# Attention with two queues of block moves: from four and twelve per head to eight and eight

## The reference

```python
def attend_blocks(q, k_all, v_all):              # 16 heads of 128, 4 key heads, 256 queries, 512 keys
    def one(qblk):
        s = jnp.einsum('bqkgd,btkd->bkgqt', qblk, k_all).astype(jnp.float32) * scale
        p = jax.nn.softmax(s, axis=-1).astype(v_all.dtype)
        return jnp.einsum('bkgqt,btkd->bqkgd', p, v_all)
    ...
    y_a = (jax.nn.sigmoid(o_a) * h * jax.nn.silu(z_a)) @ w_ba
    y_b = (o_attn * jax.nn.silu(z_b)) @ w_bb
    return (jax.nn.sigmoid(g_a) * y_a + jax.nn.sigmoid(g_b) * y_b) @ w_out
```

## Time and profile before

| | |
|---|---|
| median of 3 runs | 3128.25 us (3126.66 to 3133.57) |
| the profiled execution's own time | 3128.57 us |
| its span (first to last instruction) | 3126.6 us |
| busy: PE, DVE, ACT, POOL | 3104.6, 2145.0, 1464.9, 722.5 us |
| the attention's steps on PE | 2510 to 2673 us of the span |

### The profile page before, as it was taken

The page is one execution under the profiler, slowest core; times in us unless marked ns, Lnnn a source line. Parts: engine busy times, 40 slices in busy tenths (PEclk is TensorE's granted clock), DMA queues, the critical chain, the costliest instruction groups (busy, mean ns, idle before and its releaser), DMA issues.

```text
span 3126.6 us, 41616 instructions
## 1 busy us (share of the span) xinstructions
PE 3104.6 (99%) x14804; PEld 2561.7 (82%) x14804; DVE 2145.0 (69%) x2591; ACT 1464.9 (47%) x1805; POOL 722.5 (23%) x1127
## 2 busy tenths in 40 slices
PE   9999999999999999999999999999999999999998
PEld 8888888888777888888988888888888877888887
DVE  6888875556887678887786764655666866555556
ACT  5444444444337444444443545545455554445443
POOL 1111107947660301111012000000000577110000
PEclk9999999999999999999999999999999999999999
DMA  8999986556443789999888667546876777777754
GB/s 257 293 314 303 295 275 216 195 191 198 147 140 110 230 244 297 298 297 312 260 293 263 198 186 211 175 143 171 173 153 188 207 189 174 210 206 212 228 183 155
DMA packets 441565, 687.10 MB, mean 220 GB/s; under 512 B 138120, under 2 KB 146576, under 8 KB 440768
## 3 DMA queue, kind: packets, MB, share of 16 engines
q1 hardware_dynamic: 384176, 567.21, 57.8%
q0 software_dynamic: 39824, 115.72, 14.8%
q10 hardware_dynamic: 17408, 2.10, 0.5%
HBM read 647.93 MB, written 2.10 MB: 208 GB/s over the span
## 4 chain that ended last, share of the span: by engine, by line
PE 97%; DVE 1%; ACT 1%; POOL 0%; DMA 0%; issue 0%; SPq 0%; DVEq 0%; POOLq 0%; ACTq 0%
PE acc L301 25%; PE acc L303 25%; PE acc L302 25%; PE acc L1052 3%; PE pst L1052 3%; PE acc L1053 2%; PE pst L1054 2%; PE pst L1053 2%; PE acc L1054 2%; PE pst L2866 1%; PE pst L2545 1%; PE pst L2855 1%; PE pst L1682 0%; PE pst L2378 0%; PE pst L2547 0%; PE acc L324 0%
## 5 line engine op out<-in xcount | busy, mean ns | idle before, releaser
L249 DVE TENSOR_TENSOR w_lo<-w_raw,w_hi 128x1024 fp32r<-128x1024 f32 x1059 | 1312.1, 1246 | 807.8 <-ACT w_hi L242 800.5
L242 ACT ACTIVATE w_hi<-w_raw 128x1024 fp32r<-128x1024 f32 x1059 | 1120.3, 1060 | 1449.3 <-PE acc L303 1080.8
L301 PE MATMUL acc<-w_hi,act_hi 128*128 128x512 f32 (+1 forms) x3360 | 1319.0, 393 | 0.5 <-DVE act_lo L401 0.3
L303 PE MATMUL acc<-w_hi,act_lo 128*128 128x512 f32 (+1 forms) x3360 | 1302.9, 388 | 0.0
L302 PE MATMUL acc<-w_lo,act_hi 128*128 128x512 f32 (+1 forms) x3360 | 1302.6, 388 | 0.0
L301 PEld LDWEIGHTS acc<-w_hi,act_hi 128*128 128x128 f32 x3360 | 631.7, 188 | 131.1 <-issue 5.3
L303 PEld LDWEIGHTS acc<-w_hi,act_lo 128*128 128x128 f32 x3360 | 631.6, 188 | 127.7
L302 PEld LDWEIGHTS acc<-w_lo,act_hi 128*128 128x128 f32 x3360 | 631.9, 188 | 125.0 <-issue 1.4
L729 POOL DMA_DIRECT2D mod_ring<-in_w_mod x160 | 113.8, 711 | 831.1 <-DVE pst L749 765.8
L749 DVE SCALAR_TENSOR_TENSOR pst<-mod_ring,c_act,pst 128x512 f32<-128x512 f32 x285 | 214.6, 753 | 6.1 <-DMA mod_ring<-in_w_mod 0.7
L1052 PE MATMUL pst<-w_hi,g_hi 128*128 128x512 f32 x344 | 134.4, 391 | 0.0
(11 more groups left out here) (477 smaller groups left out, 2539.1 us busy)
## 6 DMA issues: line engine op xcount, KB each, us to landing
w_raw<-in_w_in SPq DMA_DIRECT2D x400, 512.0 KB, 4.0
w_raw<-in_ffn_w_down SPq DMA_DIRECT2D x168, 512.0 KB, 4.4
w_raw<-in_ffn_w_gate SPq DMA_DIRECT2D x160, 512.0 KB, 5.1
w_raw<-in_ffn_w_up SPq DMA_DIRECT2D x160, 512.0 KB, 6.7
mod_ring<-in_w_mod POOLq DMA_DIRECT2D x160, 512.0 KB, 6.1
w_raw<-in_w_out SPq DMA_DIRECT2D x64, 512.0 KB, 4.1
w_raw<-in_w_branch_a SPq DMA_DIRECT2D x32, 512.0 KB, 3.8
w_raw<-in_w_branch_b SPq DMA_DIRECT2D x32, 512.0 KB, 4.5
```

The costliest lines, as they stand in the source:

```text
L242: act.activation(weight_tiles(s)[0], w_raw[:, s % SLOTS, :], ACT.Copy).then_inc(w_hi_done, 1)
L249: dve.tensor_tensor(lo, w_raw[:, s % SLOTS, :], hi.bitcast(F32), ALU.subtract).then_inc(w_lo_done, 1)
L301: pe.matmul(o, xh, wh, start=k == 0, stop=False)
L303: mm = pe.matmul(o, xl, wh, start=False, stop=k == 2 * nch - 1)
```

## The change

The table of groups per queue changes. Queue 0 is ACT's, queue 1 is POOL's; each group stands for four DMAs of a head. The semaphore targets in `A2_MOVED` follow from the table.

```diff
-        A2_GROUPS = ((3,), (0, 1, 2))
+        A2_GROUPS = ((2, 3), (0, 1))
         A2_MOVED = [16 * 4 * len(groups) for groups in A2_GROUPS]
```

## The result

| | before | after |
|---|---|---|
| median, chip of the first comparison | 3128.20 us (3126.66 to 3133.57, 4 runs) | 3151.56 us (3147.54 to 3153.15, 4 runs) |
| ratio, 95% interval | | 1.0076 (1.0064 to 1.0088) |
| a second comparison, another chip | 3126.70 us (19 runs) | 3151.45 us (4 runs), 1.0081 (1.0064 to 1.0097) |
| profiled execution: time, span | 3128.57, 3126.6 us | 3147.54, 3145.7 us |

A forecast was written before the change was run, and what follows sets the result against it. PE was taken to bound the kernel, busy 3104.6 of 3126.6 us. Opening 1.83, even part 6.56, evictions 1.84 and end 2.25 sum to 12.48 us: 3140.7 against 3128.25, range 3133.5 to 3148.5.

The forecast's parts named there:

- 0.36 + 10 x 0.62: Even part, heads 3 to 13: PE stalls 0.36 us once, then 0.62 for each head, 6.56 us in all.
- the end's 0.77: End of the stage: PE's output behind head 15's eight issues and eviction comes a further 0.77 us late.
- 5.33 from exp to rounding: ACT with eight issues: the next rounding starts 5.33 us behind exp, in place of 2.70 with four.
- the hole in the opening: PE's idle 3.14 us ahead of the second output, with a slow clock behind; forecast to change owner and grow by 1.83.
- the threshold of 2.18 us: Even part: a rounding on ACT may be 2.18 us late before PE waits.
- 1.48 behind head 14: End of the stage: PE's output behind head 14's late rounding comes 1.48 us late.
- The rule of the Trainium skill that gave a rival: Rival: POOL was the bound and the opening's hole closes, winning 4.84 us, 3123.4; 5 in 100.
- The opening, +1.83 forecast: Start of the attention stage: ACT's longer rows of issues make PE's second output start 1.83 us later.
- The even part, +8.40 forecast: Heads 3 to 13: stalls of 6.56 us, plus 1.84 for the evictions behind heads 7 and 11.
- at its most, 0.737: Upper bound on ACT's price of an issue: 0.737 us each, near 4.8 us more in all, 3145.5.
- The end, +2.25 forecast: Last outputs of the stage: 1.48 us behind head 14 and 0.77 behind head 15, together 2.25.
- The rival of a clock that falls again and again: Each of 13 later stalls slows PE's clock: 22 us more, 3163; 9 in 100 together with dearer issues.

The follow-up runs named there:

- e3: Kernel before, with six of a head's moves issued on ACT and ten on POOL: 3129.87 us, ratio 1.0011.
- e5: Kernel before (four and twelve), with four chained copies on ACT behind its four issues of a head: 3132.95 us, ratio 1.0024.
- e4: Changed kernel's eight and eight, but ACT's eight in two lots of four, one behind each exp of a head's two steps: 3128.05 us, ratio 1.0007.
- e10: The changed kernel, unchanged, run and profiled a second time: 3151.45 us, ratio 1.0081; its profiled execution took 3148.46 us.
- e7: Changed kernel's eight and eight, with two banks of scores and two of outputs in place of three and one: 3143.04 us, ratio 1.0059.
- e15: The changed kernel, unchanged, a third profiled execution: 3144.96 us.
- e13: The kernel before, unchanged, a third profiled execution: 3128.78 us.
- e9: The kernel before, unchanged, run and profiled a second time: 3126.27 us, ratio 1.0004; its profiled execution took 3124.42 us.
- e14: The kernel before, unchanged, a fourth profiled execution: 3126.39 us.
- e12: Changed kernel's eight and eight, ACT's eight in two lots of four, and outputs seven steps behind the scores, not six: 3128.00 us, ratio 1.0004.

## Why the prediction was wrong in size

**What failed.** The median of before came out as assumed, 3128.20. The changed kernel was put at 3140.7 and took 3151.56, 10.9 more. In its first profiled execution (3147.54, against 3141.05) the pieces are over the forecast by 0.7 (opening, 38.26 against 35.72 + 1.83), 4.9 (even part) and 2.3 (end, each with its term added to before's), and the rest of the program was 1.4 shorter. So the terms that failed are the even part's "0.36 + 10 x 0.62" and the end's 0.77: what a row of eight issues costs was taken from medians (5.33 from exp to rounding; measured 5.44 to 6.45 without an eviction), and head 15's row was left where it had stood. The other 4.0 us lie in executions without a trace.

**Right.** PE stands still once in two steps, released by line 2886; POOL was not the bound (its bursts are 4.62 us, and it waits 4.0 to 6.5 us between them); the hole in the opening doesn't close, but changes its owner from the moves to ACT; the threshold of 2.18 us (e3, e5); the head distance of 9.6 (9.64 to 9.82 where no long issue, eviction or slow stretch comes in, but for 9.94 twice and 10.17 once); 1.48 behind head 14 (1.43). The rule of the Trainium skill that gave a rival (Perfetto Trace Analysis, DMA Optimizations) says that balancing DMAs over the engines may help where descriptor generation is the bottleneck. POOL, which waits 3.61 us in a head, was not, and nothing was won: laid out with the gap in mind (e4) the balanced version is not told from before, and without it the change is 0.8% slower.

**The opening, +1.83 forecast, +5.0 measured.** The sum was made against one execution, and its opening, 35.72, was the longest of four. Against that execution the change costs 2.54, near the forecast. The step that failed in the table of means is the base: I took DVE's wait of 4.49 as a property of the kernel. It hangs on one landing, and the earlier trace rows had the spread, 1.8 to 6.4 us, on which I had only based that heads would land in time. The base explains 2.1 (35.72 less the mean of 33.59) of the 3.2 that are missing between the means (5.00 - 1.83), the term itself 1.0. It doesn't explain why the time of the changed kernel lies above the range.

**The even part, +8.40 forecast, +11.59 measured.** The term "0.36 + 10 x 0.62" took 5.33 from exp to rounding, and the loop was right. But the gap was too short, and long single issues I had priced by a median. Head by head, against a distance of 9.62 (10.54 with an eviction), the three executions after are 4.7, 2.4 and 2.0 us over. The rows with an issue over 0.9 us make 3.1, 1.7 and 0.6 of that (five, three and one such issue), the slow stretch of the first execution 0.8, and the rest, 0.8, 0.7 and 1.4, is spread over the other rows, whose gaps without an eviction are 5.44 to 5.97 in place of 5.33. A row of four has 2.18 us in which a long issue vanishes; a row of eight has nothing left, so nearly all of it goes into the time: in e10 an issue of 1.51 lengthens the gap to 6.45. The bound "at its most, 0.737" was read from a profile with 64 issues in which none was long.

**The end, +2.25 forecast, +4.42 measured.** The term 0.77 behind head 15 moved the output's due time by head 14's 1.48, but left the start of the eight issues where it had been. They wait for `a2_turned`, and the last turn stands behind a late rounding: they start at 2669.90, 1.67 behind a rounding of 2668.23, where before it was 0.08. The rest is again a long issue (1.20 in place of 0.64 in the first execution, 1.19 in e10) in the row of 5.92. The two make 1.59 + 0.56 = 2.15, which is the miss of 2.94 - 0.77 = 2.17.

**The explanation of the stall** was half right. I had put it down to PE's wait for line 2886, with the next maximum late as a consequence. e7 shows the loop through line 2898 and exp to be the cause, and PE's wait one of two places where it surfaces.

**The clock.** The rival of a clock that falls again and again did not come true: of the 32 stalls in the even parts of the three executions one was followed by a slow stretch (1.98 us, in the first), though e15 has one of 1.93 that wasn't. The Trainium skill (TensorE: Matmul & The Clock Gate, A second HAM failure mode) tells of a kernel whose frequent short idle times brought the clock down again and again. Here, with a stall about every 10 us, it came down once, so the trace does not agree but for that one case.

**Still open.** The profiled executions differ by 19.95 us in their times, the medians by 23.4 and 24.8. In both comparisons the profiled execution of after was the fastest of its runs (3147.54 against 3150.59 to 3153.15; 3148.46 against 3151.43 to 3151.80). Some 3 to 4 us therefore lie in executions that no trace here shows; more long issues would do it, but that is only argued. Open too is why some moves land in 2.7 and others in 6.2 us.

## What to carry to other kernels

A DMA issue is work of the engine that issues it, though the profile doesn't count it as busy: before giving issues to an engine, lay the row of them into its gap between one urgent instruction and the next, and follow the loop that closes over the other engines; past the slack every tenth, and nearly all of every odd long issue, is paid. The same issues in two lots, one in each gap, cost nothing that could be told. And profile the kernel before more than once, before a wait that hangs on one landing is taken for its property.

## What the runs showed of the hardware

- A DMA issue on ACT takes 0.59 to 0.70 us in most cases, and now and then 0.9 to 1.5 (13 of 384 in three executions), each of these beside an instruction fetch of 8 or 16 KB. POOL's issues of the same moves stay at 582 to 594 ns in all 384.
- Moves of 32 KB land 1.8 to 6.4 us after their issue in the execution on record; the median rose from 3.0 to 4.1 us with eight and eight. By queue it was 4.3 us for ACT's and 2.9 for POOL's before, and 4.2 and 3.9 after.
- Six chained copies of 128x280 on ACT take 2.78 us, 0.46 each.
- PE's clock was at its lower level for 3.4 us behind an idle time of 3.14 us (e13: 2.53), and for 6.8 us around one of 5.23. It never was in the stage of e9 (0.48), e14 (1.01), e4 (1.85) and e12 (1.73), but once for 3.4 us behind 1.98. The length of the idle time alone doesn't decide it: behind the 2.79 us at the end of the changed kernel's stage it stayed up.
